# Four adaLN blocks and the order of the first two heads: moving work of DVE, ACT and SyncE in a hybrid transformer block

## What is computed

```python
def reference(x, c, positions, w_ada, b_ada, ...):
    mod = silu(c) @ w_ada + b_ada
    sh1, sc1, gt1, sh2, sc2, gt2 = split(mod, 6)
    h = rmsnorm(x, g_norm1) * (1.0 + sc1) + sh1
    x = x + gt1 * hybrid_mixer(h, ...)
    h = rmsnorm(x, g_norm2) * (1.0 + sc2) + sh2
    x = x + gt2 * swiglu(h, w_gate, w_up, w_down)
    return rmsnorm(x, g_final)

def hybrid_mixer(h, ...):
    mq, mk, mv, mo, gpre, aq, ak, av = split(h @ w_in)
    mq, mk = split(silu(conv5(concat(mq, mk))))
    h_fwd, h_bwd = mlstm(mq, mk, mv, gates), mlstm_reversed(...)
    m_out = sigmoid(mo) * layernorm_per_head(h_fwd + h_bwd) * g_mlstm_out
    a_out = rmsnorm(windowed_gqa(rope(aq), rope(ak), av, sink), g_attn_out)
    return concat(m_out, a_out) @ w_out
```

## Time and profile before

| | us |
|---|---|
| median of 3 runs | 2321.93 |
| lowest and highest | 2320.53, 2322.32 |
| the profiled execution, whole | 2321.62 |
| its span in the trace | 2319.7 |
| PE busy in it | 2254.2 (97%) |
| DVE busy | 1526.9 (66%) |
| ACT busy | 887.1 (38%) |
| POOL busy | 232.1 (10%) |
| mean granted clock of PE | 0.982 of full |

### The profile page before, as it was taken

The page is one execution under the profiler, slowest core; times in us unless marked ns, Lnnn a source line. Parts: engine busy times, 40 slices in busy tenths (PEclk is TensorE's granted clock), DMA queues, the critical chain, the costliest instruction groups (busy, mean ns, idle before and its releaser), DMA issues.

```text
span 2319.7 us, 27076 instructions
## 1 busy us (share of the span) xinstructions
PE 2254.2 (97%) x10486; PEld 1871.2 (81%) x10486; DVE 1526.9 (66%) x1735; ACT 887.1 (38%) x1047; POOL 232.1 (10%) x90
## 2 busy tenths in 40 slices
PE   5999999999998999999999999999999999999998
PEld 4777878888876788788888888888888888888887
DVE  6958667574758557667787878787878544444444
ACT  4333232323245322444444444444444433343333
POOL 0001334333320012100000000000000001010001
PEclk8998999999999999999999999999999999999999
DMA  9943444444542567324443444444443855554553
GB/s 361 374 126 123 149 164 146 145 160 167 182 156 81 191 258 277 109 91 145 163 157 133 145 154 161 137 136 154 163 145 127 324 202 185 195 200 182 185 194 129
DMA packets 188198, 404.43 MB, mean 174 GB/s; under 512 B 11328, under 2 KB 67920, under 8 KB 172496
## 3 DMA queue, kind: packets, MB, share of 16 engines
q1 hardware_dynamic: 175088, 387.10, 47.0%
q10 hardware_dynamic: 13024, 16.13, 2.0%
HBM read 383.27 MB, written 19.92 MB: 174 GB/s over the span
## 4 chain that ended last, share of the span: by engine, by line
PE 87%; DVE 6%; issue 2%; DMA 1%; ACT 1%; POOL 1%; SPq 0%; POOLq 0%; DVEq 0%; ACTq 0%
PE ps L1790 26%; PE ps L1792 26%; PE ps L1791 26%; DVE acc L1097 1%; PE ps L1949 1%; PE ps L2236 1%; DVE acc L1338 1%; DMA fr<-in_w_ada 1%; DMA araw<-in_w_ada 1%; PE ps L1962 1%; PE ps L1960 1%; POOL wlo L536 1%; DVE qk L1307 1%; PE ps L1822 1%; PE ps L1881 0%
## 5 line engine op out<-in xcount | busy, mean ns | idle before, releaser
L926 ACT ACTIVATE whi<-wraw 128x1024 fp32r<-128x1024 f32 x200 | 211.0, 1060 | 276.7 <-DVE wraw L1613 153.4
L1594 DVE TENSOR_TENSOR wlo<-wraw,whi 128x1024 fp32r<-128x1024 f32 x200 | 240.7, 1220 | 76.9 <-ACT whi L926 76.9
L1790 PE MATMUL ps<-d_hi,whi 128*128 128x512 f32 (+1 forms) x736 | 280.4, 381 | 0.0
L1792 PE MATMUL ps<-d_hi,wlo 128*128 128x512 f32 (+1 forms) x736 | 279.9, 380 | 0.0
L1791 PE MATMUL ps<-d_lo,whi 128*128 128x512 f32 (+1 forms) x736 | 279.8, 380 | 0.0
L1790 PE MATMUL ps<-h_hi,whi 128*128 128x512 f32 x680 | 271.5, 399 | 2.5 <-POOL wlo L536 2.5
L1792 PE MATMUL ps<-h_hi,wlo 128*128 128x512 f32 x680 | 266.9, 393 | 0.0
L1791 PE MATMUL ps<-h_lo,whi 128*128 128x512 f32 x680 | 266.6, 392 | 0.0
L1706 DVE TENSOR_TENSOR d_lo<-d_raw,d_hi 128x2048 fp32r<-128x2048 f32 (+1 forms) x44 | 99.8, 2267 | 243.2 <-ACT d_hi L993 243.2
L1790 PE MATMUL ps<-whi,sk_hi 128*128 128x512 f32 x640 | 251.0, 392 | 0.0
L1792 PE MATMUL ps<-whi,sk_lo 128*128 128x512 f32 x640 | 249.7, 390 | 0.0
(11 more groups left out here) (332 smaller groups left out, 3876.1 us busy)
## 6 DMA issues: line engine op xcount, KB each, us to landing
araw<-in_w_ada SPq DMA_DIRECT2D x64, 1024.0 KB, 5.9
wraw<-in_w_gate SPq DMA_DIRECT2D x88, 512.0 KB, 3.8
wraw<-in_w_up SPq DMA_DIRECT2D x88, 512.0 KB, 4.7
d_raw<-aT_keep SPq DMA_DIRECT2D x44, 1024.0 KB, 4.8
wraw<-in_w_down SPq DMA_DIRECT2D x44, 1024.0 KB, 7.1
wraw<-in_w_in SPq DMA_DIRECT2D x38, 1024.0 KB, 5.3
acc<-in_w_up SPq DMA_DIRECT2D x40, 512.0 KB, 5.5
wraw<-in_w_out SPq DMA_DIRECT2D x16, 1024.0 KB, 8.1
```

The source lines that it names most:

```text
L926: A(EHI[e % 4], src, ACT.Copy).then_inc(uhi_ok, 1)
L1594: V_.tensor_tensor(ELO[e % 4], src, EHI[e % 4].bitcast(F32), ALU.subtract).then_inc(ulo_ok, 1)
L1790: pe.matmul(o, w_hi, m_hi, start=first, stop=False)
L1792: return pe.matmul(o, w_lo, m_hi, start=False, stop=last)
```

## The change

- Quarter 3's pair 7: its four loads stand at the same place of SP's queue as in the other quarters (behind ring pair 2), and its 16 products stand between the matmuls of front slot 5.
- The gates' projection: 6 of 16 row tiles ahead of front slot 6, 10 behind slot 7 (before: 12 and 4).
- DVE does conv(0,0) ahead of `gates_in`. The copy of the gate columns moves from DVE to ACT, between the two sigmoids of j=6 of head 0.
- Head 1 (and head 1 alone, the other one that is written out and not looped): the sigmoids of j=5 move from the end of that step to behind weight split 19 in j=6.
- adaLN blocks 0 to 3 move from the attention units to output-projection slots 2, 2, 3 and 3, and their loads, and those behind them, follow by the rule of the table.
- `scale_gain(4, C_G2)` moves from the tail to slot 8.

```diff
@@ -336,8 +336,8 @@
 
             return 7 if u % 2 and u < TWO_BANKS else 3
 
-        LATE_OP = [0, 1, 2, 3, 4, 4, 5, 5, 7, 7, 8, 8, 9, 9, 10, 10, 11, 11, 12, 12, 13, 13, 14, 15]
-        LATE_LD = [0, 1, 2, 3, 4, 4] + [LATE_OP[n - 2] + 2 for n in range(6, 24)]
+        LATE_OP = [2, 2, 3, 3, 4, 4, 5, 5, 7, 7, 8, 8, 9, 9, 10, 10, 11, 11, 12, 12, 13, 13, 14, 15]
+        LATE_LD = [0, 1] + [LATE_OP[n - 2] + 2 for n in range(2, 24)]
 
         def c_bank(u):
 
@@ -393,7 +393,7 @@
                     sp.dma_start(wgraw[:], w_in[0, :, COL_G:COL_G + GATES].rearrange("(k p) c -> p k c", p=P)).then_inc(wg_ld, 16)
                 if pair == 3 or (pair == 6 and quarter < 3):
                     front_slot(2 * quarter + (pair == 6))
-                if pair == (PE_AT if quarter < 3 else 6):
+                if pair == PE_AT:
                     if quarter:
                         sp.wait_ge(ada_pe, quarter)
                     for k in range(2):
@@ -709,9 +709,9 @@
                 A(R[0:64, :], ROPE[k][64:P, :], ACT.Copy)
                 A(R[64:P, :], ROPE[k][0:64, :], ACT.Copy).then_inc(rot_ok, 1)
 
-            def conv_sigmoids(h, j):
-
-                for i in range(2):
+            def conv_sigmoids(h, j, which=(0, 1)):
+
+                for i in which:
                     t = 2 * (j - 5) + i
                     act.wait_ge(conv_pre, h * 4 + (t + 1))
                     A(Pt[:, i, 0:4, :].rearrange("p a b -> p (a b)"), qk[:, t, :], ACT.Sigmoid).then_inc(conv_sig, 1)
@@ -741,7 +741,10 @@
                 o_gate(0, "head")
                 act.wait_ge(w_used, 24)
                 hi(13, 1, 11)
-                conv_sigmoids(0, 6)
+                conv_sigmoids(0, 6, (0,))
+                act.wait_ge(gcol_ps, 1)
+                A(acol[:], ps[5][:, 0:14 * GR], ACT.Copy).then_inc(gcol_sb, 1)
+                conv_sigmoids(0, 6, (1,))
                 exp_minus_m()
                 turned_v(0)
 
@@ -754,6 +757,8 @@
                     if not isinstance(h, int) or 13 < s2 < NB:
                         act.wait_ge(w_used, h * 16 + (8 + 2 * j))
                         hi(s2, (3 + j) % 2, h * 4 + ((3 + j) // 2 + (3 + j) % 2 + 5))
+                    if j == 6 and kind == "head" and isinstance(h, int):
+                        conv_sigmoids(h, 5)
                     if j == 0 and not (isinstance(h, int) and h == 1):
                         o_gate(m, "tail" if kind == "end" else "head")
                     if j == 0 and mixing:
@@ -776,7 +781,7 @@
                         act.wait_ge(ht_ps, h)
                         for i in range(2):
                             evac(vT[:, i, :], i, tile_done(h, 2, i))
-                    if kind == "head" and j in (5, 6):
+                    if kind == "head" and (j == 6 or j == 5 and not isinstance(h, int)):
                         conv_sigmoids(h, j)
                     if kind == "tail" and j in (5, 6):
                         if j == 5:
@@ -1225,10 +1230,6 @@
                             ch.link(V_.tensor_scalar(arow[0:32, k, :], aa[0:32, chunk(j)], off[0:32], None, ALU.add))
                             ch.link(V_.tensor_scalar(arow[32:64, k, :], back, off[32:64], None, ALU.add))
                 V_.tensor_copy(arow[0:1, 0, 0:1], arow[0:1, 0, 0:1]).then_inc(arow_ok, 1)
-
-            def gate_columns():
-                dve.wait_ge(gcol_ps, 1)
-                V_.tensor_copy(acol[:], ps[5][:, 0:14 * GR]).then_inc(gcol_sb, 1)
 
             def select(h):
 
@@ -1387,8 +1388,8 @@
                         ada_take(h // 2, h // 2 + 1, 6)
 
             front_lo(9, SLOT)
+            conv(0, 0)
             gates_in()
-            conv(0, 0)
             front_lo(10, SLOT)
             conv(0, 1)
             silu(0, 0)
@@ -1396,7 +1397,6 @@
             gate_rows_()
             select(0)
             conv_pair(0, 2)
-            gate_columns()
             trig()
             trig_round(2048.0)
             trig_round(1.0)
@@ -1462,8 +1462,6 @@
                     ada_b(i % 2, 32 + i, 16 * (14 + 16 + 4))
                 elif u in ROPE_AT:
                     rope(ROPE_AT[u])
-                elif u in (12, 16, 20, 24):
-                    ada_late(u // 4 - 3)
                 elif u == 11:
                     early_lo(1)
                 elif u == 26:
@@ -1496,7 +1494,10 @@
                     dve.wait_ge(modp_ok, 5)
                 if v == 7:
                     ada_take(3, 4, 4)
-                for n in range(4, 24):
+                if v == 8:
+                    dve.wait_ge(modp_ok, 7)
+                    ch.link(scale_gain(4, C_G2))
+                for n in range(24):
                     if LATE_OP[n] == v:
                         ada_late(n)
                 if v % 4 == 2 and v >= 4:
@@ -1545,7 +1546,7 @@
                 last = V_.tensor_scalar(sqt[:, 0, tb * P:(tb + 1) * P], ident[:], rs[:, tb:tb + 1], None, ALU.mult)
             last.then_inc(n_dg, 1)
             dve.wait_ge(modp_ok, 8)
-            ch.link(scale_gain(4, C_G2))
+
             def scaled(k):
 
                 dve.wait_ge(x_sp[0], 48)
@@ -1893,17 +1894,15 @@
 
             for quarter in range(1, 4):
                 front_slot(2 * quarter - 2)
-                front_slot(2 * quarter - 1, quarter if quarter < 3 else None)
+                front_slot(2 * quarter - 1, quarter)
                 ada_columns(quarter)
                 if quarter < 3:
                     keep_busy()
-            for j in range(8):
-                ada_direct(3, j)
             pe.wait_ge(wlo_ok, 8)
-            gates_of(range(12))
+            gates_of(range(6))
             front_slot(6)
             front_slot(7)
-            gates_of(range(12, KT)).then_inc(w_used, 2)
+            gates_of(range(6, KT)).then_inc(w_used, 2)
 
             def slot(h, j):
                 par, g, kk = (1 + j) % 2, j // 2, j % 2
```

## The result

The changed kernel takes 2303.87 us in the median of four runs (2303.43 to 2305.12), the kernel before, run beside it, 2322.12. The ratio is 0.9916, 95% interval 0.9904 to 0.9928, which is −17 to −22 us. The profiled execution took 2305.12 us.

The account below looks back on a forecast made before the run. PE, busy 97% of the span, was taken as the bound, so only its waits and low-clock time could be gained. −5.0 − 2.9 + 1.7 − 6.3 = −12.5 us gave 2309.4 us, range 2303.5 to 2314.0.

Parts of the forecast that it names:

- Front, −5.0: Front: direct products inside slot 5 and fewer gate products ahead start slot 6 7.8 us earlier, 2.8 paid back later; −5.0 us.
- the clock stays at 1.00 there: Front, quarter 3 after the change: full clock expected as in quarter 2; a fall would cost +0.8 us.
- Gate columns, −2.9: Head 0: with ACT copying the gate columns, PE starts at 204.3 instead of 207.21 us, the clock still falling; −2.9 us.
- The rival of a clock that stays up: Behind the gate columns: clock stays full, the term is −7.3 instead of −2.9, total 2305.0 us; chance 0.24.
- Head 1, +1.7: Head 1: POOL's earlier split holds up DVE's convolutions and delays m, so slot (2,0) starts later; +1.7 us.
- Attention, −6.3: Attention: without four adaLN blocks in DVE's queue, PE's 7.6 us of idle falls to 1.3; −6.3 us.
- my sign, below 1.5 us in sum: Attention: PE's waits on aout and prT were to come out below 1.5 us in sum.
- Where the blocks went, conv(0,0) and scale_gain, 0: Output-projection slots 2 and 3, head 0 and slot 8: the moved blocks, conv(0,0) and scale_gain were to cost 0.
- two stretches at the lower clock which the change can move: Only two low-clock stretches counted: behind the front's fourth quarter (0.52) and behind the gate columns (0.51).
- the rival by which one swallows the other's gain: Head 1: PE waits for DVE's convolutions and m, giving back the front and gate-column gains; 2317 us, chance 0.05.

Follow-up runs that it names:

- w1: The changed kernel with the 14 gate-column products spread between the products of the slot ahead, in place of a block behind it: 2306.47 us, ratio 0.9923.
- vw: The changed kernel with both edits, m ahead of the convolutions in head 1 and the gate-column products spread: 2302.58 us, ratio 0.9904.
- a2: The changed kernel again, same code, on another chip: 2305.74 us, ratio 0.9916.
- a3: The changed kernel a third time, same code, on the same chip as a2: 2304.52 us, ratio 0.9915.
- v1: The changed kernel with m written ahead of head 1's two convolutions and ACT's copy of v between the two sigmoids: 2301.22 us, ratio 0.9899.
- v1b: The same program as v1, run a second time on that chip: 2300.09 us, ratio 0.9895.
- p4_head1: The changed kernel with head 1's sigmoids back ahead of weight split 19: 2307.22 us, ratio 0.9921.
- p4b: The same kernel as p4_head1, run again on the chip of a2 and a3: 2306.61 us, ratio 0.9917.

## Why the prediction was wrong, point by point

Behind each term stands what the traces measured; for the front and the falls all fourteen traces are used.

- **Front, −5.0.** In the first pair of traces the term came out as forecast: column sums to gate columns 156.97 us before and 151.85 after, −5.1. Part of that was luck, two errors that cancel: quarter 3's column sums start 78.8 us behind quarter 0's, where the working has 80.7, and slot 6 starts 6.4 us behind them, where it has 4.6, since the clock fell. The step that failed is the base: I took 136.28 and a low clock that ends at 132.4 for the kernel's time. Over four traces of this front the stretch from the column sums to the gate columns is 157.0 to 159.9 us (mean 159.0), over eight of the new one 150.0 to 152.7 (mean 151.5): −7.5. The difference lies behind quarter 3's column sums. From them to slot 6 the trace that I read has 14.1 us and the three others 17.3 to 17.4; the new front has 4.8 us in five traces and 6.2 to 6.4 in the five in which the clock fell. What stands there before the change are the 16 direct products and the 24 narrow gate products, and how much of them falls under the lower clock is the scatter. The change takes the 16 away.
  I had also said that the clock stays at 1.00 there, because quarter 2 is the same code. That was misread. The window of the earlier trace rows from 70.5 us on lies behind slot 1, that is behind quarter 1; behind slot 3, where quarter 2 has the same pattern, the same trace shows half the clock, and eleven of the thirteen others have a fall there too:

```profile
98.10:104.90 6.80, 6.80 (x16) 4.50 (x17) 5.49 (x12) 5.28 (x7) 0.00 (x0) 0.50 1.05 385
```

- **Gate columns, −2.9.** Measured −3.0 in every trace that has the block (7.02 or 7.03 us with DVE's copy, 3.99 with ACT's), and the clock fell behind it in all of them. The rival of a clock that stays up was wrong: it fell with 0.7 us of waiting as with 3.7, and stayed up only in w1 and vw, which have neither the block nor the wait. The 0.7 us and the block were not parted. The fall was mostly shorter with ACT's copy: from the turn of v to slot (2,0) it is 95.0 to 96.4 us in the four traces with DVE's copy and 94.4 or 94.5 in the three with ACT's and the old order of head 1, some 1.2 us more that the term doesn't have.
- **Head 1, +1.7.** Measured +1.6 between the end of slot (1,7) and slot (2,0), by the mechanism forecast: POOL under the convolution, m late, 4.5 us of waiting. The +1.6 of the table's row is the same number by chance, since that row moves with the clock too: a2 and a3 have 96.07 and 96.03 us in it, as much as the kernel before. The rule of the Trainium skill ("SBUF — State Buffer", section "Who interferes with whom") that a DVE operation with at most one SBUF input outside the fast modes runs beside GpSimd is what v1 shows with m, 1.40 us. The convolution's 4.82 and 3.51 us agree with the lock that the Trainium skill describes there.
- **Attention, −6.3.** Measured −6.9 with the other parts away, −8.4 in the first pair; the 1.5 between them are a fall of the clock near 620 us that was shorter after the change. The size came near by two errors that offset each other: in the window of the earlier trace rows the two waits went from 7.6 us to 3.1, and not to the 1.3 that I had reckoned with (my sign, below 1.5 us in sum, failed), and 2.0 us came from outside of the window, which I hadn't counted. Over the whole span they went from 11.5 us to 5.0.
- **Where the blocks went, conv(0,0) and scale_gain, 0.** Measured 0: DVE's idle time took the blocks in; from the select products to the gate columns PE takes 40.2 us with conv(0,0) moved or not, and the tail ahead of the feed-forward shows no new wait.
- **What I left out, −3.3.** The step that failed is the sentence that there are two stretches at the lower clock which the change can move. The trace of before has, beside those near 98 and 303 us, four more from the end of the heads on that I had not put into the argument: near 620, 760, 828 and 940 us. The changed kernel lacks the one at 828 (−3.3 us) in three traces of three. Here are those of before, in the order of time:

```profile
619.00:627.50 8.50, 8.50 (x34) 7.26 (x34) 7.41 (x9) 3.31 (x6) 4.31 (x1) 0.60 0.72 261
759.00:767.00 8.00, 5.39 (x25) 4.65 (x25) 5.96 (x8) 4.24 (x6) 1.01 (x1) 0.79 0.00 0
...
940.00:948.00 8.00, 7.39 (x23) 5.46 (x24) 1.67 (x8) 1.78 (x2) 1.01 (x1) 0.57 0.31 127
```

The terms as measured, −7.5 − 3.0 + 1.6 − 6.9 − 3.3, make −19.1, inside the measured −17 to −22. Row by row, three traces of the changed kernel less two of the kernel before give on average +0.4, −6.6, −3.0, +1.0, +1.3, −8.4 and −3.4, before rounding −18.6 in sum. The mean granted clock of the span went from 0.982 and 0.983 to 0.987 in all three. The three parts run alone sum to −20 (−9.8, −3.0, −7.4), within some 5 us, so the parts add up as far as this can tell, and the rival by which one swallows the other's gain is out. The range was too narrow by a cause that is plain now: the bounds were those of the waits, and none was kept for the clock, whose falls come and go by 2 to 5 us a run.

What stays open is why the fall near 820 us is missing in the changed kernel three times, and so whether its 3.3 us are the change's work at all. Ten of the fourteen traces have it; the fourth without it is v1b. It is there with the front, the gate columns or the adaLN blocks alone, and with all but head 1's order (p4_head1, p4b). Head 1's order alone was not run, but w1 has that order and has the fall. It isn't bound to the program (v1 and v1b), and in the 30 us ahead of the short products the instructions of PE, DVE and ACT in a3 and p4b start at the same distance from them, within 0.04 us; only their arrival differs, by 1.2 us. That the moment of arrival decides is a guess; no run here moved that alone.

The version with m ahead in head 1 is the best one run: 2301.22 and 2300.09 us in two sessions on one chip, against 2305.74 and 2304.52 for the changed kernel beside it, some 4.5 us and 0.2% less, at intervals of the ratios that still overlap.

## What to carry to other kernels

Sum up what a change gives at the joints of the program, from several traces of the same kernel and not from one, and price each block of very short products with the products behind it at both clocks: here the front's block, 2.5 us more than forecast, and the one near 828 us, 3.3 us, stand for 5.8 us of 18. Before moving work of GpSimd to an earlier time, look at which VectorE operation it will lie beside; here the one that reads PSUM ran on, and the convolution's first step, which works on SBUF alone, stood until GpSimd was through. And order the operation that another engine waits for ahead of those that nobody needs yet: here it gave 4.2 us between slot (1,7) and slot (2,0), where the change's own reordering cost 1.6.

## What had not been expected of the hardware

- A block of 32 one-column products, with no wait near it, is followed by some 7 us at half clock (3.3 us lost) in one execution and by full clock in another of the same program (v1 and v1b).
- A short product of 36 columns costs 0.24 us in a block of its own and 0.54 us between products of 512 columns.
- A VectorE operation with one PSUM and one SBUF operand (m) takes 0.7 us (1.40 for two) whether or not GpSimd works beside it; one with a single operand, from SBUF to SBUF (the convolution's first step), takes 0.54 us alone and up to 4.82 beside GpSimd.
